# A float32 FFN up-projection written as seven block products for two output tiles, with the weight sums on GpSimd

## What is computed

```python
h2 = modulate(h_res, p['g_ffn'], sh2, sc2)
up = h2 @ p['w_up']                                  # 1024 -> 5632 channels
buf = jnp.concatenate([st_conv[layer].astype(F32), up], axis=1)
conv = causal_dwconv(buf, p['conv_w'], p['conv_b'], l)   # width 3, per channel
a_ff, b_ff = jnp.split(conv, 2, axis=-1)
h_res = h_res + gt2[:, None, :] * ((jax.nn.gelu(a_ff) * b_ff) @ p['w_down'])
out_conv.append(buf[:, -(CONV_W - 1):])
```

## Time and profile before

| | us |
|---|---|
| median of three runs | 2586.6 |
| lowest, highest run | 2580.49, 2586.95 |
| the profiled execution, device time | 2590.91 |
| its span in the trace, first to last instruction | 2589.2 |
| TensorE busy | 2364.4 (91%) |
| VectorE busy | 878.4 (34%) |
| ScalarE busy | 453.5 (18%) |
| GpSimd busy | 158.3 (6%) |

### The profile page before, as it was taken

One profiled execution on the slowest core, in us unless ns is written; L12 is line 12 of the kernel. 1 busy time (PEld: TensorE's weight loads), 2 busy tenths in 40 slices (PEclk: granted clock), 3 DMA queues, 4 the chain that ended last, 5 costly groups with the idle time before them and its releaser, 6 DMA issues.

```text
span 2589.2 us, 40401 instructions
## 1 busy us (share of the span) xinstructions
PE 2364.4 (91%) x18161; PEld 1542.4 (60%) x18161; DVE 878.4 (34%) x1399; ACT 453.5 (18%) x895; POOL 158.3 (6%) x269
## 2 busy tenths in 40 slices
PE   5998999979879988888889997999999999999994
PEld 3665666656556556557466654666656666665663
DVE  3953432243153253243324233333321013333222
ACT  4114111141141131132210002111110001111002
POOL 2700000010001001001000000000000000000001
PEclk8999999999999989999889998999999999999997
DMA  6101223200210210210244110111000111111001
GB/s 223 67 21 30 84 77 109 74 16 17 71 48 15 74 47 12 77 44 12 104 133 132 50 63 4 33 43 59 25 25 25 58 34 34 34 36 40 21 21 68
DMA packets 107212, 139.81 MB, mean 54 GB/s; under 512 B 14755, under 2 KB 77720, under 8 KB 107025
## 3 DMA queue, kind: packets, MB, share of 16 engines
q1 hardware_dynamic: 92352, 115.38, 13.6%
q10 hardware_dynamic: 10992, 15.21, 1.6%
q0 software_dynamic: 3696, 6.64, 0.9%
HBM read 117.59 MB, written 19.61 MB: 53 GB/s over the span
## 4 chain that ended last, share of the span: by engine, by line
PE 82%; DVE 8%; ACT 4%; DMA 2%; issue 2%; ACTq 0%; SPq 0%; DVEq 0%; POOL 0%; POOLq 0%
PE ps L632 81%; DVE arena L1754 3%; DVE arena L1757 2%; PE ps L636 1%; DMA W<-in_w_in_dram 1%; ACT Y L1504 1%; DMA arena<-in_x_prompt_dram 1%; DMA Y<-in_x_prompt_dram 0%; DVE hT L1757 0%; DVE hT L1754 0%; DVE arena L2122 0%; ACT arena L1429 0%; DVE s5v L1754 0%; DMA out_dram<-arena 0%; ACT arena L1382 0%
## 5 line engine op out<-in xcount | busy, mean ns | idle before, releaser
L632 PE MATMUL ps<-hT,W 128*128 128x352 f32 x4368 | 1368.0, 471 | 40.5 <-DVE Y L1754 14.3
L632 PEld LDWEIGHTS ps<-hT,W 128*128 128x128 f32 x4368 | 829.9, 193 | 497.4 <-issue 55.3
L632 PE MATMUL ps<-arena,W 128*128 128x352 f32 x1440 | 432.0, 463 | 14.7 <-DVE arena L1754 11.9
L632 PEld LDWEIGHTS ps<-arena,W 128*128 128x128 f32 x1440 | 276.1, 192 | 170.1 <-DVE arena L1754 12.5
L632 PE MATMUL ps<-arena 64*64 64x64 f32 (+5 forms) x9224 | 276.3, 230 | 36.5 <-issue 21.9
L632 PEld LDWEIGHTS ps<-arena 64*64 64x64 f32 (+2 forms) x9224 | 224.9, 135 | 134.6 <-issue 86.1
L1382 ACT ACTIVATE Y<-ps 128x352 f32<-128x352 f32 (+3 forms) x220 | 69.7, 349 | 715.4 <-PE ps L632 536.6
L2301 DVE TENSOR_SCALAR Y<-Y,PAR 128x1024 f32<-128x1024 f32 x88 | 49.0, 557 | 426.3 <-ACT Y L1382 424.7
L1754 DVE TENSOR_TENSOR arena<-arena 128x1056 f32<-128x1056 f32 (+6 forms) x181 | 166.8, 922 | 64.2 <-PE ps L632 49.2
L1754 DVE TENSOR_TENSOR arena<-ps,arena 128x512 f32<-128x512 f32 (+4 forms) x124 | 93.2, 751 | 274.8 <-PE ps L632 222.7
L1382 ACT ACTIVATE arena<-ps 128x512 f32<-128x512 f32 (+7 forms) x179 | 106.1, 608 | 432.7 <-PE ps L632 228.4
(11 more groups left out here) (253 smaller groups left out, 960.7 us busy)
## 6 DMA issues: line engine op xcount, KB each, us to landing
W<-in_w_ada_dram SPq DMA_DIRECT2D x12, 2048.0 KB, 9.3
W<-in_w_up_dram SPq DMA_DIRECT2D x22, 1024.0 KB, 7.1
gates<-arena ACTq DMA_DIRECT2D x72, 176.0 KB, 1.8
arena<-gates SPq DMA_DIRECT2D x24, 528.0 KB, 3.5
W<-in_w_in_dram SPq DMA_DIRECT2D x6, 2048.0 KB, 8.3
W<-in_w_in_dram SPq DMA_DIRECT2D x13, 512.0 KB, 5.8
W<-in_w_down_dram SPq DMA_DIRECT2D x4, 1536.0 KB, 6.5
W<-in_w_in_dram SPq DMA_DIRECT2D x5, 1024.0 KB, 6.4
```

The lines of the kernel that those rows point to most:

```text
L632: return nc.tensor.matmul(out, lhsT, rhs, start=start, stop=stop, skip_group_check=True)
```

## The change

Two output tiles of the same kind (`a` tiles p, p+1 for r even; `b` tiles for r odd) are computed together; r counts such pairs, 0 to 21, as p counted hidden tiles. The 256 x 1024 weights are cut into 2 x 2 blocks, and so is the 1024 x 1056 input (halves of k, and 2 x 528 columns). `pair(r)` makes the four blocks of the result out of seven products instead of eight (the Winograd form of Strassen's scheme). Each product is 2 x 264 columns over four k, 8 instructions, in two neighbouring PSUM banks; a pair takes three such slots, rotating. Products 1 and 3 sum in one slot, and 5 and 7 in another, with reads of the slot between the two.

- **Sums of weights.** GpSimd makes S1, S2, A11 - A21 (written over A21 in W) and S4 of pair r+1 while pair r runs: four adds of 128 x 512, into `S124`, which has two sets.
- **Sums of inputs.** Once, before the first pair: BT1, BT2 and BT4 on DVE, BT3 on GpSimd, each 128 x 4 x 528. BT4 goes over the place of B12 in `hT`. ACT may read the first product only after these (`mg_ready`).
- **Combining.** ACT copies the slot of product 1, and later of products 1+3, into the tile buffers (two copies of 528 columns per pair). DVE adds the other products to them: five adds of 528 columns that read PSUM.
- **Convolution.** The same operations, one pair later than its products, and in between the five adds; `a` tiles go straight into `FFh`, and gelu works there in place.
- **Residual.** `arena` columns 0 to 6335 now hold BT1 to BT3, so `xT` doesn't stay. GpSimd stores it to DRAM (`xres`) during the output projection; in the first half's down-projection SP loads tile after tile into a ring of two, and GpSimd stores them again; in the second half all eight tiles are loaded back at the second weight chunk, and DVE waits for all.
- **Start of the down-projection.** PE waits for all but the last two hidden tiles, and for those when it comes to them in the first column group.
- A few semaphores of earlier stages are merged (`u0_done` into `wy_done`, `kraw_ready` and `cums_ready` into `mixed`), with the same waits.

```diff
-        out += [("up", m, 4 * G) for m in range(m0, m1, 2)]
+        out += [("up", m, 2 * PRODUCTS) for m in range(m0, m1, 2)]
...
+        BT2, BT3, BT1 = carve(0, 4, HT), carve(2112, 4, HT), carve(4224, 4, HT)
+        B11, B12, B21, B22 = (hT[:, 4 * a:4 * a + 4, HT * b:HT * (b + 1)] for a in range(2) for b in range(2))
+        BT4 = B12
+        xring = carve(6336, 2, T)
...
+        def slots(r):
+            return [2 * ((x - r) % 3) for x in range(3)]
...
+                elif k == "down" and c[1] == 1:
+                    for m in range(KT):
+                        sp.wait_ge(sem(f"x_put{m % 2}"), 64)
+                        sp.dma_start(xT[:, m, :], xres[m]).then_inc(sem(f"x_in{m % 2}"), 16)
...
+            def sums(r):
+                i = index[("up", 2 * (r // 2))]
+                pool.wait_ge(sem(f"w_in{i % 2}"), loads[i])
+                if r >= 2:
+                    pool.wait_ge(sem("gemm_done"), product(r - 2, 7))
+                A11, A12, A21, A22 = blocks(r)
+                S1, S2, S4 = S124[r % 2]
+                for x, (o, a, b, op) in enumerate(((S1, A21, A22, ADD), (S2, S1, A11, SUB), (A21, A11, A21, SUB),
+                                                   (S4, A12, S2, SUB))):
+                    pool.tensor_tensor(o, a, b, op).then_inc(sem("s_sums"), 1)
+                    pool.wait_ge(sem("s_sums"), 4 * r + x + 1)
...
+            def multiply(b, A, B, first=True, last=True):
+                for g in range(2):
+                    for k in range(4):
+                        m = mm(pb[b + g][:, 0:HG], A[:, k, :], B[:, k, HG * g:HG * (g + 1)], first and k == 0, last and k == 3)
+                m.then_inc(sem("gemm_done"), 1)
...
+                x, y, z = slots(r)
+                take(x, x + 1)
+                multiply(x, A11, B11, True, False)
...
+                multiply(y, S2, BT2)
+                pe.wait_ge(sem("p12_ev"), 2 * r + 1)
+                multiply(x, A12, B21, False, True)
...
+                multiply(z, A21, BT3)
+                pe.wait_ge(sem("comb"), 5 * r + 1)
+                multiply(y, S1, BT1, True, False)
+                pe.wait_ge(sem("p12_ev"), 2 * r + 2)
...
+                multiply(x, A22, BT4)
+                pe.wait_ge(sem("s_sums"), 4 * r + 4)
+                pe.wait_ge(sem("comb"), 5 * r + 3)
+                multiply(y, S4, B22, False, True)
...
-                    for q in range(2):
-                        for s in range(2):
-                            gemm(wslot(i, 2048 * s, 8, 256), P * q, 8, h, "u_in")
-                    if n:
-                        last_rows(n - 1)
-                pe.wait_ge(sem("ff_ready"), m1)
+                    pair(2 * n + 1)
+                pe.wait_ge(sem("ff_ready"), m1 - 2)
...
+            step(tt(BT1, B12, B11, SUB), "h_ready")
+            step(tt(BT2, B22, BT1, SUB), "h_ready")
+            dve.wait_ge(sem("t3_ready"), 1)
+            step(tt(BT4, BT2, B21, SUB), "h_ready")
...
+                    if r > m0:
+                        conv(r - 1, 0)
+                    dve.wait_ge(sem("p12_ev"), 2 * r + 1)
+                    combined(r, 2, c12, c12, y, ADD)
+                    if r > m0:
+                        conv(r - 1, 1)
+                    combined(r, 4, c21, c12, z, ADD)
+                    combined(r, 5, c22, c21, y, ADD)
+                    combined(r, 6, c21, c21, x, SUB)
+                    combined(r, 7, c12, c12, y, ADD)
```

More of the change, by code:

```diff
@@ new lines, in state_rows @@
+            def state_rows(r):
+                n, s = r // 2, r % 2
+                if n and not s:
+                    rows_out(n - 1)
+                for a in range(2):
+                    u = Uab[2 * s + a]
+                    src = 2 * s + a
+                    copy(cob[:, src, 0:2], u[:, TP:TP + 2])
+                    copy(cob[:, src, 2:18].rearrange("p (n r) -> p n r", r=2), dec_of(u)[:, :, 4:6])\
+                        .then_inc(sem("cob_made"), 1)
+                act.wait_ge(sem("cob_made"), 2 * (r + 1))
@@ new lines, in gelu @@
+            def gelu(p):
+                act.wait_ge(sem("conv_a"), p + 1)
+                f = FFh[:, p - (0 if p < HALVES[0][1] else HALVES[1][0]), :]
+                nc.scalar.activation(f, f, ACT.Gelu_apprx_tanh).then_inc(sem("gelu_done"), 1)
+            act.wait_ge(sem("mg_ready"), KT + 1)
+            for m0, m1 in HALVES:
+                for r in range(m0, m1):
+                    x, y, z = slots(r)
+                    turned = r > m0 and r % 2 == 1
+                    if r > m0:
+                        decode_rows(r - 1)
+                    act.wait_ge(sem("gemm_done"), product(r, 1))
+                    if r >= 2:
+                        act.wait_ge(sem("u_used"), 2 * (r - 1))
+                    copy(corner(r, 0, 1), ps[:, x:x + 2, 0:HG]).then_inc(sem("p12_ev"), 1)
+                    if r > m0:
+                        state_rows(r - 1)
+                    if turned:
+                        gelu(r - 1)
+                    act.wait_ge(sem("gemm_done"), product(r, 3))
+                    copy(corner(r, 0, 0), ps[:, x:x + 2, 0:HG]).then_inc(sem("p12_ev"), 1)
+                    if turned:
+                        gelu(r)
+                decode_rows(m1 - 1)
+                state_rows(m1 - 1)
@@ L2252, in _, with residual @@
             res = [RING_OUT]
-            def residual(base, gate, n_norm=None):
+            def residual(base, gate, n_norm=None, place=lambda m: xT[:, m, :]):
                 for m_ in range(KT):
+                    home = place(m_)
                     for g in range(G):
@@ new lines, in _, with ring_place @@
+                conv(m1 - 1, 0)
+                conv(m1 - 1, 1)
+                if half == 0:
+                    def ring_place(m):
+                        dve.wait_ge(sem(f"x_in{m % 2}"), 144 + 16 * (m // 2 + 1))
+                        return xring[:, m % 2, :]
+                    residual(signals[index[("down", (m0, 0))]], 40, None, ring_place)
+                else:
+                    for k in range(2):
+                        dve.wait_ge(sem(f"x_in{k}"), 272)
+                    residual(signals[index[("down", (m0, 0))]], 40, 2)
```

233 lines of the change are left out of this document (139 added, 94 removed).

## The result

| | us |
|---|---|
| median before (4 runs) | 2586.77 |
| median after (4 runs, 2514.49 to 2521.28) | 2518.84 |
| ratio, 95% interval | 0.9741, 0.9720 to 0.9761 |
| profiled execution after: device time, span | 2514.49, 2512.7 |

The change makes the kernel 2.6% faster. 2515.7 us was predicted, in a range of 2503 to 2546.

The account below looks back on a forecast made before the run. TensorE, busy for 91% of the span, was taken to bound the kernel. 2590.9 - 76.1 + 4.5 + 0.7 = 2520.0 us for a profiled execution; the median, 4.3 us lower, gives 2515.7 us, range 2503 to 2546.

Parts of the forecast that it names:

- TensorE bounds, and a product left out is time left out: In the FFN TensorE has no gaps, so dropping one of eight products saves its time: 76.1 us over 22 pairs.
- The pass: One TensorE pass of 264 columns in the FFN's products takes 0.2236 us, with ends 0.2186 and 0.235.
- rival B: TensorE's weight loads stand still 0.2 us at each product's start: 31 us more, 2547 us; chance 0.12.
- Waits inside a pair: ACT, DVE and GpSimd work in each pair hides behind TensorE; first DVE add ready by 12.3 us, needed at 14.3.
- the lock: GpSimd and DVE exclude each other at their shared SBUF ports; four GpSimd adds, 5.1 us, counted one after the other with DVE's convolution.
- The start of the FFN: Making the input sums delays the first products, and the clock may fall again: +4.5 us, bounds 0 and 8.
- The down-projections: At their starts TensorE waits for the last two tiles, 5.6 and 6.8 us; both together +0.7 us.
- The residual's trips: Storing the residual to DRAM and loading it back in the down-projections stays hidden: cost 0.
- The sum: Whole kernel: 2590.9 - 76.1 + 4.5 + 0.7 = 2520.0 us profiled; median 4.3 us lower, 2515.7.
- C: GpSimd's adds take 1.9 us instead of 1.27, delaying DVE's adds in every second pair: 2527 to 2538 us; chance 0.13.
- D: Slower: GpSimd adds at 3.5 us each make TensorE's fifth product wait in each pair, near 2668 us; chance 0.04.
- E: Passes don't run at their columns' rate; a pair stays near 28.5 us and the time within noise; chance 0.05.

## Why the prediction was right, step by step

- **TensorE bounds, and a product left out is time left out.** Right; the eighth product put back costs 79.5 us where 78.3 was worked out from its passes.
- **The pass.** I took 0.2236 us and it is 0.2225; the ends of 0.2186 and 0.235 were both off. I had read 0.0036 us on top of the columns from 57.00 / 192, but that length includes the tail of the last pass (a product of 16 passes is 3.72 us long and the next begins after 3.56). The start-to-start time of products, 3.56 us for 16, leaves 0.0025. The same slip is in both kernels, so it cancels: 3.46 us a pair was predicted, 6.97 / 2 = 3.48 measured. Most of the "quarter microsecond for twelve waits" that I held against rival B was that tail too, and the 0.133 us of the nine-column passes contains such tails as well, so it is an upper bound; rival B fell by the trace after, where seven products follow each other every 3.56 us with all their waits.
- **Waits inside a pair.** All hide. After `b` tiles the first add was said to end at 12.3 us at worst and ends 10.3 us after product 1 starts (1684.02 against 1673.71); it is needed at 14.2. The term that was mis-sized is the lock: 5.1 us by adding GpSimd's durations, 2.9 us measured (9.30 us for the convolution, its multiplication and the add, against 6.39 for the same operations right behind, from 1684.07 to 1690.46, with GpSimd idle). The steps that I named as exposed were those with two inputs in SBUF; those with one were held up too (1.12 against 0.81 us, 1.13 against 0.30).
- **The start of the FFN.** +4.5 us was predicted with ends of 0 and 8. The first pair takes 1597.52 - 1563.89 = 33.6 us against 24.9 for a pair at the full clock, 8.7 more; before, a cold start cost 2.53. So +6.2. The wait of 3.0 us and the second cold stretch were both among what I named. In seven later profiles with the same start, product 3 begins 14.25 to 14.52 us after product 1, and here 15.73: 6.2 is the high end of this term, and some 5 us is usual. The repeats' FFN was no shorter for it (949.4 and 949.0), since the down-projections took longer there.
- **The down-projections.** 5.6 and 6.8 us of standing were predicted; 5.50 and 6.35 came. The sum was right in part by luck: in the first half 0.96 us of it is a wait for the bank in which product 7 stood, which I had overlooked, and TensorE's own ten tiles covered more of DVE's work in return. And my +0.7 should have been +0.5 by my own terms, 5.6 + 6.8 against 2 x 5.95.
- **The residual's trips.** Hidden, as predicted. In the second half DVE waited for the loads until 2326.84 us, 17.4 after the weights ahead of them were issued, where I had said 22 to 28; TensorE was never held up by them.
- **The sum.** -76.7 + 6.2 - 0.05 = -70.5, against 71.0 measured in the FFN and 70.9 predicted. The spans of the two profiles differ by 76.5, and the 5.5 beyond the 71.0 are the part ahead of the FFN, which began that much earlier. The medians differ by 67.9; no profile shows where the other 3 us are, but the FFN began anywhere between 1560.6 and 1572.1 us in the profiles, so it is well within what that part varies by. My last step, taking the profiled execution's 4.3 us over the median along unchanged, was of no use: the changed kernel's profiled execution was 4.3 us *under* its median. That the median was hit within 3.1 us is therefore in part luck; the 70.9 us for the FFN is what the working earned, and there too the errors of the terms, 0.6 and 0.75 us one way and 1.7 the other, nearly cancel.
- **Rivals.** B, C and D were possible by mechanism and not in this kernel as it is. C and D share one, which twelve adds brought out. E, that the chip might not run the passes at their columns' rate, fell by the 112 passes of a pair in 25.13 us (row 1852.05).

## What to carry to other kernels

Where one engine bounds a stage without a gap, price a change by that engine's instruction count times its start-to-start time, and check for each new wait only that the chain behind it ends before the need; here the slack was 4 us in 25, and the extra work of two other engines cost nothing inside the pairs. It did cost some 5 us once, at the start, where there was no slack. The seams between stages are where the rest lies: at each, ask which work of the bounding engine doesn't need the late operand, and put it first (16 us here for issuing 60 passes in one half and 48 in the other ahead of the wait), and keep the two engines that hold each other up from working at the same critical moment (4 to 6 us).

## What was not expected of the hardware

- GpSimd and DVE take turns cheaper than their durations say: 2.19 us for a DVE step of 1.285 and a GpSimd add of 1.266 together. But a short DVE instruction suffers most for its length: 32 columns, 0.30 us alone, take 1.13. And one of 2112 columns behind an equally long one of GpSimd's takes 6.68 instead of 2.36. That GpSimd holds the lock from start to end, as the Trainium skill has it (SBUF, "State Buffer", section "Who interferes with whom"), fits the last number; by the first, some 0.35 us of the recorded durations of a turn lie outside the lock, in one engine's or in the other's, which no run here tells.
- With eight and with twelve GpSimd adds DVE's first convolution, with the multiplication and the add behind it, takes the same 11.43 us: an instruction of DVE is held up once at most, so more GpSimd work only reaches further down DVE's queue.
- Making the weight sums on GpSimd costs DVE as much busy time as making them itself: 32.31 against 31.97 us per chunk.
